# A two-layer decoder trunk: the mean of squares of the second layer's head norms as two split matmuls

## The reference, cut to what matters

```python
y = xf * lax.rsqrt(jnp.mean(xf * xf, axis=-1, keepdims=True) + NORM_EPS)
...
q = _rope(_rmsnorm(q, q_norm_g), cos, sin)
k = _rope(_rmsnorm(k, k_norm_g), cos, sin)
ki = _rope(_rmsnorm(ki, ik_norm_g), cos_i, sin_i)
```

## Time and profile before

| | us |
|---|---|
| median of 3 runs | 2219.75 (2219.74 to 2220.39) |
| the profiled execution | 2219.86 |
| its span | 2218.1 |
| TensorE busy | 2211.4 |
| VectorE busy | 1494.5 |
| ScalarE busy | 1177.1 |
| GpSimd busy | 3.0 |

### The profile page before, as it was taken

How to read it: one execution, slowest core, us unless ns; L and a number is a source line. 1 busy time by engine, 2 the same in 40 slices (tenths; PEclk the granted TensorE clock), 3 DMA queues, 4 the chain that set the end, 5 groups by cost and what they waited for, 6 DMA issues and landing times. The chain is left out here.

```text
span 2218.1 us, 35419 instructions
## 1 busy us (share of the span) xinstructions
PE 2211.4 (100%) x12790; PEld 1947.8 (88%) x12790; DVE 1494.5 (67%) x1774; ACT 1177.1 (53%) x1409; POOL 3.0 (0%) x10
## 2 busy tenths in 40 slices
PE   9999999999999999999999999999999999999999
PEld 8888898888888888888899888888888888888888
DVE  7666556677777777555578888667777777774444
ACT  7565555555555555444455466555555555553332
POOL 0000000000000000000000000000000000000000
PEclk9999999999999999999999999999999999999999
DMA  7555545555565555555566544455565656565654
GB/s 270 168 170 173 171 162 180 195 184 193 185 196 182 191 187 194 192 190 190 190 206 198 178 156 141 161 183 189 180 199 179 198 180 199 180 199 199 200 197 136
DMA packets 113686, 411.51 MB, mean 186 GB/s; under 512 B 12752, under 2 KB 13392, under 8 KB 113616
## 3 DMA queue, kind: packets, MB, share of 16 engines
q1 hardware_dynamic: 112608, 406.96, 55.9%
q10 hardware_dynamic: 576, 1.97, 0.2%
q0 software_dynamic: 432, 1.57, 0.2%
HBM read 408.36 MB, written 2.10 MB: 185 GB/s over the span
## 5 line engine op out<-in xcount | busy, mean ns | idle before, releaser
L716 DVE TENSOR_TENSOR w_lo<-raw,w_hi 128x1024 fp32r<-128x1024 f32 x769 | 935.2, 1224 | 670.9 <-ACT w_hi L276 665.1
L1273 PE MATMUL psum<-xg,w_hi 128*128 128x512 f32 (+1 forms) x3936 | 1358.5, 391 | 1.2 <-DVE xg L727 0.9
L276 ACT CAST w_hi<-raw 128x1024 fp32r<-128x1024 f32 x770 | 803.0, 1049 | 767.6 <-PE psum L1273 764.8
L1273 PE MATMUL psum<-xg,w_lo 128*128 128x256 f32 (+1 forms) x3920 | 1089.4, 278 | 0.0
L1273 PEld LDWEIGHTS psum<-xg,w_hi 128*128 128x128 f32 x3936 | 735.8, 187 | 156.6 <-issue 3.3
L1273 PEld LDWEIGHTS psum<-xg,w_lo 128*128 128x128 f32 x3920 | 741.2, 189 | 2.7 <-issue 2.2
L1273 PE MATMUL psum<-hid,w_hi 128*128 128x512 f32 x1408 | 488.2, 391 | 0.0
L1273 PE MATMUL psum<-hid,w_lo 128*128 128x256 f32 x1408 | 394.2, 280 | 0.0
L1273 PEld LDWEIGHTS psum<-hid,w_hi 128*128 128x128 f32 x1408 | 263.3, 187 | 57.7
L1273 PEld LDWEIGHTS psum<-hid,w_lo 128*128 128x128 f32 x1408 | 266.1, 189 | 0.0
L1273 PE MATMUL psum<-att,w_hi 128*128 128x512 f32 x512 | 178.8, 393 | 0.0
(11 more groups left out here) (166 smaller groups left out, 888.4 us busy)
## 6 DMA issues: line engine op xcount, KB each, us to landing
raw<-w_all SPq DMA_DIRECT2D x770, 512.0 KB, 3.4
xres<-x_in SPq DMA_DIRECT2D x3, 512.0 KB, 9.5
cst<-consts_in ACTq DMA_DIRECT2D x2, 768.0 KB, 6.0
out_t<-xres POOLq DMA_DIRECT2D x3, 512.0 KB, 3.7
raw<-w_all SPq DMA_DIRECT2D x2, 256.0 KB, 3.5
xres<-x_in SPq DMA_DIRECT2D x2, 256.0 KB, 4.5
out_t<-xres SPq DMA_DIRECT2D x4, 128.0 KB, 1.8
vecs<-vecs_in ACTq DMA_DIRECT2D x1, 354.0 KB, 7.9
```

The source lines that it names most:

```text
L276: act.copy(w_hi[:, c % RING, :], raw[:, c % RING, :]).then_inc(hi_ready, 1)
L716: dve.tensor_tensor(w_lo[:, c % RING, :], raw[:, c % RING, :], f32(w_hi[:, c % RING, :]), ALU.subtract).then_inc(lo_ready, 1)
L1273: return pe.matmul(o, lhsT, rhs, start=start, stop=True, skip_group_check=True)
```

## The change

`usq` becomes an fp32r buffer with two parts. ACT squares twice: once unrounded into `rsn`, which is free until the Ln writes it, and once rounded into part 0 of `usq`. GpSimd subtracts the two and writes the remainder into part 1. TensorE multiplies part 0 and part 1 by an fp32r copy of the averaging matrix, made once by ACT, and both products are accumulated in the same PSUM bank. TensorE now waits for GpSimd where it waited for ACT. ACT's squaring waits in addition for the mean of the block before.

```diff
-        usq = sb("usq", [P, 2, T], F32, l1)
+        usq = sb("usq", [P, 2, 2, T], F32R, l1)
+        avg_r = sb("avg_r", [P, P], F32R, l1)
@@ gpsimd, behind the memsets
+            for nb in range(11):
+                nh = 2 if nb else 1
+                pool.wait_ge(rb_sq, 2 * nb + 2)
+                pool.tensor_tensor(usq[:, 1, 0:nh, :], rsn[:, 0:nh, :], f32(usq[:, 0, 0:nh, :]), ALU.subtract).then_inc(usq_ready, 1)
@@ scalar, evac
                     act.wait_ge(rb_u, nb + 1)
-                    act.activation(usq[:, 0:nh, :], u[:, 0:nh, :], ACT.Square).then_inc(rb_sq, 1)
+                    if not (isinstance(nb, int) and nb == 0):
+                        act.wait_ge(ms_ready, nb)
+                    act.activation(rsn[:, 0:nh, :], u[:, 0:nh, :], ACT.Square).then_inc(rb_sq, 1)
+                    act.activation(usq[:, 0, 0:nh, :], u[:, 0:nh, :], ACT.Square).then_inc(rb_sq, 1)
@@ scalar, once, in the first block of layer 1
+                    act.copy(avg_r[:, :], avg_h).then_inc(avg_rounded, 1)
@@ tensor, mean_squares
-                pe.wait_ge(rb_sq, nb + 1)
-                if not (isinstance(nb, int) and nb == 0):
+                pe.wait_ge(usq_ready, nb + 1)
+                if isinstance(nb, int) and nb == 0:
+                    pe.wait_ge(avg_rounded, 1)
+                else:
                     pe.wait_ge(rsn_ready, nb)
-                mm(psum[:, 5, 0:nh * T], avg_h, usq[:, 0:nh, :], True).then_inc(ms_ready, 1)
+                mm(psum[:, 5, 0:nh * T], avg_r[:, :], usq[:, 0, 0:nh, :], True)
+                mm(psum[:, 5, 0:nh * T], avg_r[:, :], usq[:, 1, 0:nh, :]).then_inc(ms_ready, 1)
```

More of the change, by code:

```diff
@@ L195, in build @@
         rb_copied, rb_sum, rb_u, rb_sq = sem("rb_copied"), sem("rb_sum"), sem("rb_u"), sem("rb_sq")
+        usq_ready, avg_rounded = sem("usq_ready"), sem("avg_rounded")
         ms_ready, ln_ready, rsn_ready = sem("ms_ready"), sem("ln_ready"), sem("rsn_ready")
```

## The result

| | before | after |
|---|---|---|
| median of 7 runs, us | 2219.75 (2219.17 to 2220.39) | 2228.04 (2227.16 to 2228.62) |
| profiled execution | 2219.86 | 2228.19 |
| span | 2218.1 | 2226.4 |

The kernel became slower by 0.37%, a ratio of 1.0037 [1.0028, 1.0046]. I had forecast 2220.7, no change, with a range that ended at 2227.

The account below looks back on a forecast made before the run. TensorE's queue was taken to bound the kernel. The terms 0.45 + 1.53 + 0.87 - 0.40 - 2.0 - 0.25 + 0.65 = +0.85 us on 2219.86 gave 2220.7, range 2217.5 to 2227.

Parts of the forecast that it names:

- The bound: Whole kernel: TensorE, busy 2211.4 of 2218.1 us, sets the time; a microsecond off its queue is one off the kernel.
- the places of the stalls: TensorE waits for GpSimd's remainder at nb 1, 2 and 3 only: 0.8, 1.9 and 1.3 us.
- the chain of 2.59 us: From the first squaring's start through second squaring, subtraction, hops and weight load to TensorE's matmul: 2.59 us.
- the subtraction: GpSimd's remainder of the squares: taken as 1.2 us, half for nb 0, between bounds of 0.52 and 1.37.
- the terms of nb 0, 1, 2 and 4 to 9: Forecast +0.65 at nb 0, +0.45 at nb 1, +1.53 at nb 2, -0.40 at nb 4, -2.0 for nb 5 to 9.
- the step of nb 3: At nb 3: GpSimd waits 0.3 us for DVE's operation in hand; stall 1.27, less 0.40 saved: +0.87 us.
- rival C: Clock falls after each of three stalls (nb 1 to 3) for some 4 us: +6, 2226.7; chance 0.05.
- rival A: GpSimd gets no turn until DVE pauses, at nb 0 (+6.0) and nb 3 (+5.9): +11.2, 2231.0; chance 0.14.
- the step of nb 10: At nb 10: transposes behind it already wait for DVE's probabilities, so 0.25 of the 0.40 saving counts: -0.25 us.
- The upper bound of the subtraction: GpSimd's subtraction as three streams in sequence plus 0.1 us estimated fixed cost: at most 1.37 us.

Follow-up runs that it names:

- e5: Kernel before with only nb 3 in the split form, ACT keeping its second squaring in the loop: 2225.54 us, ratio 1.0025.
- e6: Kernel after, with DVE waiting before the second half of the selection until GpSimd's subtraction of nb 3 is done: 2225.52 us, ratio 1.0026.
- e7: Kernel before plus 60 consecutive GpSimd subtractions of 128x384 beside layer 0's MLP, their results unused: 2251.4 us, ratio 1.0132.
- e4: Kernel before with only nb 4 to 9 split; ACT still squares twice at nb 10: 2219.45 us, ratio 0.9998.
- e8: Kernel after with nb 0 to 3 in the old form and the negation of the maxima on ACT instead of DVE: 2218.73 us, ratio 0.9993.
- e11: Kernel before plus one fp32r matmul of 256 columns ahead of nb 10's mean, its result overwritten: 2221.81 us, ratio 1.0009.
- e9: Kernel before with its buffers at the places of the kernel after, no instruction changed: 2220.24 us, ratio 1.0002.

## Why the prediction was wrong

**What held.** The bound (TensorE's queue), the places of the stalls, the chain of 2.59 us (2.57), the subtraction (1.2 against 1.29 us), and the terms of nb 0, 1, 2 and 4 to 9: together 0.23 forecast and 0.20 measured. At nb 0 the 0.44 is the time for which DVE stood: its pair L1038 took 1.57 us for 1.12. At nb 1 and 2 two sizes missed and in part cancelled. The mean started 0.8 and 1.7 us late (0.85 and 1.93 forecast), and behind the stall the split form saved some 0.3 us by the starts, not 0.40. That the four terms agree so well in sum is partly luck.

**What failed: the step of nb 3.** It read "DVE is in a row of two-input operations over SBUF here, and I let GpSimd wait 0.3 us for the one in hand". GpSimd was passed over at six ends of DVE's instructions, 2.9 us of its 4.22, so the stall was 3.73 instead of 1.27; and behind it the clock fell, which my rival C had only behind three stalls, and for some 4 us each, which no row gave (here about 3.4). +0.87 became +5.17, which e5 shows alone and e6 shows to be DVE's doing. I had rival A for this place (the mean near 1292.8; it came at 1293.18), but only together with nb 0, at 0.14. That the times lie so close is luck: A had GpSimd wait for a pause of DVE's, and by then DVE was 2.8 us later than before; the turn came ahead of the pause, between two rows. The two places were separate questions. At nb 0 the turn changed at the next end, at nb 3 it didn't. A at nb 3 alone, with the clock behind it, was a case of its own: with this term put right the sum is 2219.86 + 0.85 + 4.30 = 2225.0, which my range holds, and the next two terms carried the time past its end.

The Trainium skill (SBUF — State Buffer, section Who interferes with whom) says that a DVE operation with two inputs in SBUF and a GpSimd one that reads SBUF exclude each other for the whole instruction. The traces agree: 1.65 us for 0.69 at L1053, 1196 ns for 479 in e7, and 1211 for 1218 ns at L979, whose one input is in PSUM. I had that rule and drew from it that the turn changes at the next end, or only in a pause of DVE's. At nb 0 it was the next end, at nb 3 a later one, and no pause.

**What failed: the step of nb 10.** I searched DVE's queue for two-input operations only. The instruction that mattered was a `tensor_scalar` of 128x4, 0.17 us long, that the exponentials stand behind. It was held 0.85 us at each of nb 5 to 10. In the loop the slack covers this; behind the last block none does: +1.06 for the forecast -0.25. e4, without the subtraction of nb 10, and e8, which moves the negation to ACT and leaves the rest, each take the wait away. The same section of the Trainium skill counts `tensor_scalar` among the forms that can take the shared ports; 1.02 for 0.17 us in six of eight rows agrees.

**What I did not have: the rhythm.** +1.58 us where nothing waits. e11 shows that one matmul more in TensorE's stream can bring it without any part of the change. Its cause is open.

**A term without a source.** The upper bound of the subtraction, 1.37 us, rests on 0.1 us of fixed cost, which no row showed. From the three sizes measured (0.80, 1.02 and 1.28 us for 256, 384 and 512 columns) my estimate is about 0.3. The subtraction still came out within the bounds.

**The order of the errors.** 0.85 forecast + 4.30 (nb 3) + 1.31 (nb 10) + 1.58 (rhythm) + 0.34 (start) - 0.03 (the rest) = 8.35 us.

## What to carry to other kernels

Work given to an idle GpSimd can run not beside DVE's but in turns with it, whole instructions at a time: list every instruction of DVE that lies beside it, a tiny `tensor_scalar` too, and ask what stands behind each. Only the operation with an input in PSUM kept its length here. Where the receiver has under 4 us on hand and DVE works without a pause, count the run of DVE's operations as a possible delay, each such place a case of its own. A saving of 0.4 us a block on the bounding engine is worth as much as the slack of what must now come first: here it was kept at the six blocks with slack and lost at the five without.

## What the runs showed of the hardware

- GpSimd's subtraction of two float32 tiles takes 1.26 to 1.30 us for 128x512 and 1.02 for 128x384, when nothing holds it. The one of 128x256 took 0.80 at nb 0, where DVE had an operation in hand for the first 0.2 us. Its memset of 128x512 took 0.52.
- The turn between GpSimd and DVE changed at the next end throughout e7, and not for six ends at nb 3 and in e5.
- A `tensor_scalar` of 128x4 on DVE took 1.01 to 1.02 us beside a subtraction, for 0.17.
- When the turn came at nb 3, DVE stood for 0.96 us.
- A stall of TensorE of 3.7 us brought the granted clock to 0.50 for some 3.4 us, at a cost of about 1.7 us (by the stretches shown: 1.30 x 0.23 + 1.50 x 0.50 + 2.00 x 0.33 = 1.71). Stalls of 0.67, 1.20 and 1.59 us left it at 1.00. The earlier trace rows have 1.00 for the first 5 us, and the kernel before stayed there; the profiled run of e9, whose instructions are the same, was at 0.51 from 9 to 16 us.
- The same stream of fp32r pairs, without a wait and at full clock, runs at 347 ns a pair or at 353 on average, and which of them it is can hang on one matmul 20 us earlier. It held for 87 us here and for over 500 us in e7.
